# Dilated attention heads: the scaling of probabilities is moved out of the joins and cut into halves, and each transpose waits for its own half

## The reference

```python
for g, (w, d) in enumerate(DIL_GROUPS):          # (128, 1), (512, 4), (2048, 16)
    q, k, v = ...                                # columns of h @ w_in
    s = einsum(qb, kn) * (E ** -0.5) + bias      # band of keys, ALiBi slopes
    m = max(s); p = exp(s - m); l = sum(p)
    o = einsum(p / l, vn); lse = m + log(l)
wts = softmax(stack(lses), axis=0)
o = sum(wts[..., None] * stack(outs), axis=0)
```

## Time and profile before

| | |
|---|---|
| median of 3 runs | 2049.86 us |
| profiled execution, its own time | 2042.99 us |
| its span, first to last instruction | 2041.3 us |
| TensorE busy | 1998.1 us, 98% |
| VectorE busy | 1095.7 us, 54% |
| ScalarE busy | 822.2 us, 40% |
| GpSimd busy | 418.8 us, 21% |
| granted TensorE clock, mean | 0.997 of full |

### The profile page before, as it was taken

How to read it: one execution, slowest core, us unless ns; L and a number is a source line. 1 busy time by engine, 2 the same in 40 slices (tenths; PEclk the granted TensorE clock), 3 DMA queues, 4 the chain that set the end, 5 groups by cost and what they waited for, 6 DMA issues and landing times. The chain is left out here.

```text
span 2041.3 us, 27385 instructions
## 1 busy us (share of the span) xinstructions
PE 1998.1 (98%) x9949; PEld 1643.8 (81%) x9949; DVE 1095.7 (54%) x1952; ACT 822.2 (40%) x1495; POOL 418.8 (21%) x343
## 2 busy tenths in 40 slices
PE   7999999999999999999999999999999999998998
PEld 4688888888888888888888788788888888796787
DVE  7744444445645645645645432697878784345312
ACT  5433323343433443443524411544454543345322
POOL 2331413323323323323310011401011010000011
PEclk8999999999999999999999999999999999999999
DMA  7331331533332332332335420411111111340422
GB/s 249 122 131 67 119 124 41 150 93 85 72 104 72 84 103 72 83 103 75 81 127 178 150 62 21 141 34 40 43 41 42 41 42 42 129 142 35 155 62 104
DMA packets 218344, 186.84 MB, mean 92 GB/s; under 512 B 9498, under 2 KB 191236, under 8 KB 217604
## 3 DMA queue, kind: packets, MB, share of 16 engines
q1 hardware_dynamic: 212960, 177.56, 28.8%
q0 software_dynamic: 4480, 6.66, 1.4%
q10 hardware_dynamic: 804, 1.33, 0.2%
HBM read 144.27 MB, written 41.25 MB: 91 GB/s over the span
## 5 line engine op out<-in xcount | busy, mean ns | idle before, releaser
L297 DVE TENSOR_TENSOR w_lo<-w_raw,w_hi 128x512 fp32r<-128x512 f32 x219 | 195.3, 892 | 166.0 <-ACT w_hi L293 165.8
L217 PE MATMUL z_ps<-b_parts,w_hi 128*128 128x512 f32 x680 | 274.8, 404 | 2.3 <-ACT g_gate L227 1.8
L219 PE MATMUL z_ps<-b_parts,w_lo 128*128 128x512 f32 x680 | 268.4, 395 | 0.0
L218 PE MATMUL z_ps<-b_parts,w_hi 128*128 128x512 f32 x680 | 268.1, 394 | 0.0
L320 PE MATMUL z_ps<-ah_hi,w_hi 128*128 128x512 f32 x512 | 209.9, 410 | 5.2 <-DVE qkv L913 2.8
L322 PE MATMUL z_ps<-ah_hi,w_lo 128*128 128x512 f32 x512 | 202.1, 395 | 0.0
L321 PE MATMUL z_ps<-ah_lo,w_hi 128*128 128x512 f32 x512 | 202.0, 394 | 0.0
L293 ACT ACTIVATE w_hi<-w_raw 128x512 fp32r<-128x512 f32 x224 | 138.4, 625 | 104.7 <-PE z_ps L322 54.0
L200 DVE TENSOR_TENSOR w_lo<-w_raw,w_hi 128x1024 fp32r<-128x1024 f32 (+1 forms) x56 | 82.1, 1466 | 153.3 <-ACT w_hi L196 153.3
L217 PEld LDWEIGHTS z_ps<-b_parts,w_hi 128*128 128x128 f32 x680 | 128.1, 188 | 35.1 <-issue 7.1
L219 PEld LDWEIGHTS z_ps<-b_parts,w_lo 128*128 128x128 f32 x680 | 127.9, 188 | 30.1
(11 more groups left out here) (507 smaller groups left out, 4471.7 us busy)
## 6 DMA issues: line engine op xcount, KB each, us to landing
w_raw<-in_a_win SPq DMA_DIRECT2D x160, 256.0 KB, 3.3
w_raw<-in_b_win SPq DMA_DIRECT2D x33, 512.0 KB, 4.0
work<-in_a_win SPq DMA_DIRECT2D x48, 256.0 KB, 5.2
v_scratch<-qkv SPq DMA_DIRECT2D x12, 1024.0 KB, 5.2
work<-v_scratch SPq DMA_DIRECT2D x16, 512.0 KB, 5.4
y_scratch<-y SPq DMA_DIRECT2D x16, 512.0 KB, 3.3
w_raw<-in_a_wout SPq DMA_DIRECT2D x8, 768.0 KB, 5.4
w_raw<-in_b_wout SPq DMA_DIRECT2D x8, 768.0 KB, 5.8
```

The lines of the kernel that those rows point to most:

```text
L217: pe.matmul(z_ps[s][:, 0:width], w_hi[slot][:, k, :], hi[k][:, tok], start=(k == 0), stop=False)
L218: pe.matmul(z_ps[s][:, 0:width], w_hi[slot][:, k, :], lo[k][:, tok], start=False, stop=False)
L219: mm = pe.matmul(z_ps[s][:, 0:width], w_lo[slot][:, k, :], hi[k][:, tok], start=False, stop=(k == nk - 1))
L297: eng.tensor_tensor(op_ring(w_lo, u), op_raw[i], op_ring(w_hi, u).bitcast(F32), ALU.subtract).then_inc(lo_op, 1)
```

## The change

The block of four residue scalings leaves `join` and becomes `scale_residues(s, half)` with two scalings; `scale_natural` gets a half too. For sequence 1 the first residue half stays in slot 27 and the second stands in slot 28; both natural halves stay in slot 30. For sequence 0 slot 31 keeps only the computation of the factors; the residue halves stand in slots 32 and 33, the natural halves in slots 34 and 35. `p_ready` counts once per half, eight times per head, and turn n waits for count n + 1 of its head.

```diff
--- before.py
+++ after.py
@@ -1273,7 +1273,7 @@
 
                         which, half = n // 2, n % 2
                         s, kind = 1 - which // 2, which % 2
-                        pe.wait_ge(p_ready, 4 * h + which + 1)
+                        pe.wait_ge(p_ready, NT * h + n + 1)
                         need(pe, pt_ready, NT * h + n)
                         for c in range(4):
                             t = TPS * (1 - kind) + 2 * half + c // 2
@@ -1498,14 +1498,16 @@
                         dve.tensor_tensor(fac[s][:], down[:], inv[:].rearrange("p (o r) -> p o r", o=1).to_broadcast([P, 2, RES]),
                                           ALU.mult).then_inc(fac_done, 1)
                         dve.wait_ge(fac_done, n + 1)
-                        for r in range(RES):
+
+                    def scale_residues(s, half):
+                        for r in range(2 * half, 2 * half + 2):
                             out = dve.tensor_scalar(x[s][:, TPS + r, :], x[s][:, TPS + r, :], fac[s][:, 1, r:r + 1], None,
                                                     ALU.mult)
                         out.then_inc(p_ready, 1)
 
-                    def scale_natural(h, s):
+                    def scale_natural(h, s, half):
                         dve.wait_ge(fac_in, 16 * ordinal(h, s) + 16)
-                        for t in range(TPS):
+                        for t in range(2 * half, 2 * half + 2):
                             out = dve.tensor_scalar(x[s][:, t, :], x[s][:, t, :], fac_nat[s][:, t:t + 1], None, ALU.mult)
                         out.then_inc(p_ready, 1)
 
@@ -1526,8 +1528,15 @@
                     def attention(h, u):
                         if u in (27, 31):
                             join(h, 1 if u == 27 else 0)
-                        if u in (30, 34):
-                            scale_natural(h, 1 if u == 30 else 0)
+                        if u in (27, 28):
+                            scale_residues(1, u - 27)
+                        if u == 30:
+                            scale_natural(h, 1, 0)
+                            scale_natural(h, 1, 1)
+                        if u in (32, 33):
+                            scale_residues(0, u - 32)
+                        if u in (34, 35):
+                            scale_natural(h, 0, u - 34)
                         if u in (36, 39):
                             finish(h, 1 if u == 36 else 0)
 
```

## The result

The changed kernel takes 2069.45 us (median of 4 runs, 2063.74 to 2077.78) against 2051.07 for the kernel before beside it: the ratio is 1.0116, 95% interval 1.0091 to 1.014. Forecast were 2047 and "no change". The range ended at 2060 and didn't hold it. It came out as rival 2 said, in mechanism and place. Between the medians the loss agrees with its 18 us (18.4); between the two profiled executions it is some 8 us more.

A forecast was written before the change was run, and what follows sets the result against it. TensorE, busy 592.08 of 595 us in the dilated heads, was taken as the bound. Waits removed (-3.6) plus new waits (+0.9) gave about -3 us, 2043.0 to 2040 for the profiled execution, median 2047; range 2039 to 2060.

The forecast's parts named there:

- rival 2: Second join: a scaling held through L1212 ahead of the z_ps eviction, 2.4 us per head, 2068 us (+0.9%); chance 12%.
- The bound and the stakes: Dilated heads: TensorE bounds; only its 4 waits for eviction L913 can be won, 3.7 us at most.
- The first join: Slots 27 to 30: two scalings move behind the next low part; TensorE gains and loses 0.
- The step that failed: Second join: the low part behind the t_ps eviction starts at 553.28, isn't held, and ends at 553.96.
- free: Second join: the low part at 553.28 runs through DMA issue L1203 unheld, -3 us in all; forecast's chance 50%.
- rival 1: Second join: low part held until 0.55 after L280, z_ps eviction ends as now, 2049.9 us, change 0; chance 30%.

The follow-up runs named there:

- mended: Changed kernel with both repairs: sequence 0's residue halves in slots 31 and 33, GpSimd's halving of the bias two weight sums later; 2040.61 us, ratio 0.9985.
- waits_only: Kernel before with only the finer count, each turn waiting for its own half, all scalings where they were; 2041.99 us, ratio 0.9974.
- first_only: Kernel before with the change in the first join (sequence 1) alone, sequence 0's scalings in slots 31 and 34; 2042.71 us, ratio 0.9982.
- sums_ahead: Changed kernel with GpSimd's weight sums L280 and L284 moved ahead of factors_out (DMA issue L1203); 2039.35 us, ratio 0.9978.
- slopes_late: Changed kernel with GpSimd's halving of the bias (L1212) two weight sums later; 2047.78 us, ratio 0.999.
- second_only: Kernel before with the change in the second join (sequence 0) alone, sequence 1's residue scalings in slot 27; 2069.04 us, ratio 1.0116.
- halves_31_33: Changed kernel with the residue halves of sequence 0 in slots 31 and 33 instead of 32 and 33; 2039.9 us, ratio 0.9983.

## Why the prediction was wrong

**The bound and the stakes: right.** The prediction put them at 3.7 us. By the starts of the turns the waits for L913 cost 4.3 us in the kernel before, and none of it is left in the variant with both repairs, where the heads follow each other at 76.15 us throughout (76.15 to 77.87 before). The times don't prove this worth: the ratios of the variants without these waits, or with 0.5 us of them, are 0.9978 to 0.9987, but `waits_only`, which keeps them, has 0.9974.

**The first join, cost 0: right.** `first_only` has no wait for a scaling.

**The step that failed** is "553.28 lies 0.16 into L1203 and 0.44 ahead of L280. I take it as not held." The low part was held in all eight heads, by L280. The row it rested on the earlier trace rows shows a low part beside a DMA issue with another DMA issue behind (L1194), and no tensor operation. What counts is what is queued behind: with no tensor operation there (`sums_ahead`) the low part took 0.68. The trace of before held the better analogue, the scaling 0.10 into L1203 that was held through L280, and I set it aside because it was of another kind of operation. The start was off too: the t_ps eviction begins 0.13 after the factors in six of eight heads and not 0.03, but the two heads with 0.03 were held as well, so that decided nothing.

The Trainium skill (SBUF — State Buffer, Who interferes with whom) says that whoever issues first keeps the port. By the recorded starts the low part was first, by 0.33 us, and lost; the measurement decides against reading the rule by recorded starts. A sum already queued seems to have its claim earlier than its row says; where exactly wasn't measured.

**From there rival 2 ran by its numbers.** It put the first scaling's end at 4.2 us after the factors (556.88 - 552.65), the second's at 6.9 and the eviction's at 7.5. In head 1 they are 4.2, 6.9 and 7.5:

```profile
559.28 1.37 DVE L1504 TENSOR_SCALAR work<-work,fac 128x256 f32<-128x256 f32 x1
```

ends at 560.65, the factors at 556.43. The reason given for the second scaling, that it starts into L1207 with L1212 right behind, was right: `slopes_late` shows that L1212 is what held it. The argument added to it, that scalings and the writing of descriptors shut each other out, isn't borne out: the scaling that started 0.14 into L1207 there took 0.34 us.

**The size: 18 us forecast for rival 2, 18.4 between the medians, 26.6 between the spans.** The waits themselves came out at 18.6 us by the starts of the turns. The half clock behind five of them adds 7.5, and no case had a price for it: that is a second term the prediction put at nothing, on a trace whose longest wait was 1.46 us and whose clock stayed full. That the medians still agree with 18 is luck: the profiled execution before is 8 us under its median, the one after sits at its own.

**The chances.** Rival 2 had 12%. Whether the low part is held had been given 5 to 3 for "free" on one row that didn't contain the neighbour in question. With the held scaling weighed as the nearest row, rival 1 and rival 2 would have had most of the chance, and the range would have reached 2068.

## What to carry to other kernels

Before moving a VectorE operation that reads SBUF, lay GpSimd's queue beside its new place: what it costs is set by the tensor operations there, one held operation per gap, and 0.6 us of work can take 4 us. Keep such operations away from between a wait and the eviction that ends it, or move GpSimd's operations, which cured it here with VectorE's order left as changed. And price a new TensorE wait of 2 to 3 us with what the clock can do behind it: in the profiled execution of the changed kernel the half clock added 7.5 us to 18.6 us of waits, in that of `second_only`, with two falls, less than 3.

## What the runs showed of the hardware that I had not expected

A GpSimd sum queued behind a DMA issue held a VectorE operation that had started 0.33 us ahead of the sum's recorded start, in all eight heads (0.43 in two of them); without a sum behind, the same DMA issue doesn't hold the low part at all (2.20 against 0.68 us).

Single executions have waits of TensorE at the start of a head that are put down to "issue": 3.2 to 4.0 us each, with the clock falling at them. In the profiled execution of `sums_ahead` (2054.29 us, while seven of its ten took 2037.5 to 2039.9) there are two; the second and the 4 us behind it:

```profile
828.51 0.79 PE L320 MATMUL z_ps<-ah_hi,w_hi 128*128 128x512 f32 x1 [4.03 <-issue]
```

```profile
829.00:833.00 4.00, 4.00 (x11) 3.03 (x11) 0.00 (x0) 0.67 (x4) 1.69 (x2) 0.50 0.12 32
```

The profiled execution of `first_only` has two as well, those of `slopes_late`, `halves_31_33` and `waits_only` have one each; those of before, the changed kernel and `mended` have none. Each kernel has one trace, so it is inferred and not shown that they come and go between executions of one kernel and make the spread of 10 us and more. Around effects of 3 us that spread is large: no order among the variants within 0.3% of the kernel before is shown. What TensorE waits for there stays open.
